# Expert outputs gate-scaled, split into a rounded head and a rounded rest, and summed into tokens by products with a 0/1 selection

## What is computed

```
logits = t @ w_router
top_val, top_idx = lax.top_k(logits, TOP_K)
gates = softmax(top_val)
combine = sum(one_hot(top_idx, N_EXPERTS) * gates[..., None], axis=1)
for e in range(N_EXPERTS):
    out = out + combine[:, e:e+1] * ((silu(t @ w_gate[e]) * (t @ w_up[e])) @ w_down[e])
x = x + out
```

## Time and profile before

| | us |
|---|---|
| three runs, median (lowest to highest) | 1259.38 (1258.75 to 1259.69) |
| the profiled execution, device time | 1258.63 |
| its span | 1256.9 |
| PE busy | 1230.5 (98%) |
| DVE busy | 574.3 (46%) |
| ACT busy | 435.2 (35%) |
| HBM rate over the span | 332 GB/s |

### The profile page before, as it was taken

One profiled execution on the slowest core, in us unless ns is written; L12 is line 12 of the kernel. 1 busy time (PEld: TensorE's weight loads), 2 busy tenths in 40 slices (PEclk: granted clock), 3 DMA queues, 4 the chain that ended last, 5 costly groups with the idle time before them and its releaser, 6 DMA issues.

```text
span 1256.9 us, 25739 instructions
## 1 busy us (share of the span) xinstructions
PE 1230.5 (98%) x11491; PEld 851.7 (68%) x11491; DVE 574.3 (46%) x898; ACT 435.2 (35%) x658; POOL 12.7 (1%) x38
## 2 busy tenths in 40 slices
PE   7999999999998999999999999999999999999997
PEld 6878888888877677777767877734366565544454
DVE  5786645556687556565765756502101011210103
ACT  6675534446564454354644544400000000000002
POOL 3000000000000000000000000000000000000000
PEclk9999999999998999999999999999999999999999
DMA  9646844165106999999999999999999999999992
GB/s 335 153 145 257 313 160 169 66 229 174 28 1 240 421 421 426 420 421 420 421 425 420 421 421 421 424 427 426 426 411 414 416 416 413 417 425 428 424 429 116
DMA packets 92773, 419.14 MB, mean 333 GB/s; under 512 B 4792, under 2 KB 8928, under 8 KB 84464
## 3 DMA queue, kind: packets, MB, share of 16 engines
q1 hardware_dynamic: 91456, 416.30, 82.1%
q0 software_dynamic: 640, 1.12, 0.4%
q10 hardware_dynamic: 560, 0.01, 0.0%
HBM read 416.37 MB, written 1.05 MB: 332 GB/s over the span
## 4 chain that ended last, share of the span: by engine, by line
PE 89%; DMA 7%; DVE 3%; ACT 1%; issue 0%; SPq 0%; DVEq 0%; ACTq 0%
PE bank L2387 26%; PE bank L2454 14%; PE bank L1983 14%; PE bank L1984 13%; PE bank L1985 13%; DMA ring<-in_moe_w_down 7%; PE bank L2321 2%; PE bank L2315 2%; DVE w_lo L1747 1%; PE bank L2049 1%; PE bank L2061 1%; PE bank L2073 1%; ACT w_hi L886 0%; DMA x<-in_x 0%; PE bank L2401 0%; PE bank L2254 0%
## 5 line engine op out<-in xcount | busy, mean ns | idle before, releaser
L1747 DVE TENSOR_TENSOR w_lo<-ring,w_hi 128x896 fp32r<-128x896 f32 (+2 forms) x192 | 201.8, 1089 | 75.2 <-ACT w_hi L886 69.7
L886 ACT ACTIVATE w_hi<-ring 128x896 fp32r<-128x896 f32 (+2 forms) x192 | 176.1, 948 | 121.8 <-PE bank L1985 95.0
L1163 ACT ACTIVATE silu_buf<-bank 128x448 f32<-128x448 f32 (+3 forms) x54 | 25.4, 485 | 407.0 <-PE bank L2387 407.0
L1983 PE MATMUL bank<-hi,act_hi 128*128 128x512 f32 (+1 forms) x400 | 154.4, 386 | 1.1 <-DVE lo L1293 1.1
L1984 PE MATMUL bank<-lo,act_hi 128*128 128x512 f32 (+1 forms) x400 | 152.5, 381 | 0.0
L1985 PE MATMUL bank<-hi,act_lo 128*128 128x512 f32 (+1 forms) x400 | 152.5, 381 | 0.0
L1770 DVE TENSOR_TENSOR silu_buf<-silu_buf,bank 128x448 f32<-128x448 f32 (+3 forms) x54 | 28.8, 550 | 233.3 <-PE bank L2387 212.1
L1293 DVE TENSOR_TENSOR lo<-raw_gu,hi 128x1024 fp32r<-128x1024 f32 x96 | 113.5, 1221 | 38.5 <-ACT hi L886 38.5
L2387 PE MATMUL bank<-ring,late_acts 128*32 128x448 f32 x1200 | 116.1, 539 | 0.0
L886 ACT ACTIVATE hi<-raw_gu 128x1024 fp32r<-128x1024 f32 x96 | 97.3, 1060 | 37.1 <-PE bank L1985 33.3
L2387 PE MATMUL bank<-ring,first_acts 128*32 128x224 f32 x2048 | 104.2, 354 | 0.6 <-ACT silu_buf L1163 0.6
(11 more groups left out here) (264 smaller groups left out, 1415.4 us busy)
## 6 DMA issues: line engine op xcount, KB each, us to landing
ring<-in_moe_w_down SPq DMA_DIRECT2D x58, 1792.0 KB, 19.6
ring<-in_moe_w_gate SPq DMA_DIRECT2D x57, 1792.0 KB, 18.0
ring<-in_moe_w_up SPq DMA_DIRECT2D x55, 1792.0 KB, 18.3
ring_after<-in_moe_w_up SPq DMA_DIRECT2D x9, 1792.0 KB, 14.4
raw_gu<-in_w_in SPq DMA_DIRECT2D x7, 2048.0 KB, 12.4
ring_after<-in_moe_w_down SPq DMA_DIRECT2D x6, 1792.0 KB, 12.2
ring_after<-in_moe_w_gate SPq DMA_DIRECT2D x6, 1792.0 KB, 13.0
raw_gu<-in_dense_w_gate SPq DMA_DIRECT2D x5, 2048.0 KB, 8.0
```

Of the source, the lines that this page charges most:

```text
L886: return nc.scalar.activation(out, in_, ACT.Copy, **kw)
L1163: nc.scalar.activation(out, gate, ACT.Silu).then_inc(e_silu_done, 1)
L1747: v.tensor_tensor(w_lo[:, n % WP, 0:b - a], flat(u)[:, a:b], w_hi[:, n % WP, 0:b - a], ALU.subtract).then_inc(w_lo_done, 1)
L1983: mm(out, ah, wh, start=start, stop=False, **kw)
```

## The change

Tile 0 of every pair, and tile 1 of pairs 0 and 1, are now *rounded* (`rounded_rows`); tile 1 of pairs 2 and 3 stays as it was. For rounded tiles:

- DVE's `gates` step compares instead of copying: `chosenT` is 1 where the transposed `gsel` is above 0, in the rounded type. The gate itself is had per slot: PE multiplies `gsel` with a column of ones (two float32 products with one column per tile), and DVE copies that column to `gate_slot`. In pair 0 this is done for both tiles at once.
- `rows_out` writes `yt_hi` = sum times gate, rounded (one tensor_scalar per old copy), waits for its own last write, and then writes `yt_lo` = sum times gate minus `yt_hi`, rounded (one scalar_tensor_tensor per old copy).
- `rows` makes two rounded products, `chosenT` by `yt_hi` and `chosenT` by `yt_lo`, instead of one float32 product.
- ACT no longer helps with the sums of the last pair's first member; DVE does all twelve pieces. ACT still helps with the second member.
- Some `extra` places of pairs 2 and 3 stand two places later. `at_buf` is smaller, and pair 2's first member keeps its activations in `late_acts` instead; no wait or instruction comes with that.

```diff
-        return ("rows", 0, n) if n < 4 else ("rows", 1, n - 6) if 6 <= n < 10 else ("gates", 0, 0) if n == 10 else None
+        return ("rows", 0, n) if n < 4 else ("rows", 1, n - 8) if 8 <= n < 12 else ("gates", 0, 0) if n == 12 else None
     if p == 3:
-        return ("rows", 0, n - 6) if 6 <= n < 10 else ("gates", n - 10, 0) if 10 <= n < 12 else None
+        return ("rows", 0, n - 8) if 8 <= n < 12 else ("gates", n - 12, 0) if 12 <= n < 14 else None
...
+def rounded_rows(p, tile):
+
+    return p < 2 or tile == 0
+
+
+def weighed_tiles(p, a):
+
+    return [t for t in ((0, 1) if p == 0 else (a,)) if rounded_rows(p, t)]
...
-                act.wait_ge(unit_used, last_unit("d", NS - 2) + 1)
-                for g in GROUPS[NP - 1, 0]:
-                    ins = last_rows_out(g)
-                ins.then_inc(y_last, 1)
...
-                        v.tensor_copy(gselT[0:m, a, :], bank[7][0:m, 0:SEQ]).then_inc(extra_out, 1)
+                        if rounded_rows(p, a):
+                            ins = v.tensor_scalar(chosenT[0:m, a, :], bank[7][0:m, 0:SEQ], 0.0, None, ALU.is_gt)
+                        else:
+                            ins = v.tensor_copy(gselT[0:m, a, :], bank[7][0:m, 0:SEQ])
+                        for tile in weighed_tiles(p, a):
+                            m, c = tile_rows(p, tile), SEQ + tile
+                            ins = v.tensor_copy(gate_slot[0:m, tile:tile + 1], bank[7][0:m, c:c + 1])
+                        ins.then_inc(extra_out, 1)
...
+                    for tile in sorted({part[1] for part in parts}):
+                        dve.wait_ge(extra_out, GATED[2 * p + tile])
+                    for rows, tile, cols, sums in parts:
+                        ins = v.tensor_scalar(yt_hi[rows, tile, cols], sums, gate_slot[rows, tile:tile + 1], None, ALU.mult)
+                    if len(parts) > 0:
+                        link(ins)
+                    for rows, tile, cols, sums in parts:
+                        ins = v.scalar_tensor_tensor(out=yt_lo[rows, tile, cols], in0=sums,
+                                                     scalar=gate_slot[rows, tile:tile + 1], in1=yt_hi[rows, tile, cols],
+                                                     op0=ALU.mult, op1=ALU.subtract)
...
-                    return mm(bank[b][:, :], gselT[0:m, tile, t * P:(t + 1) * P], yt[0:m, tile, c * 512:(c + 1) * 512],
+                    if rounded_rows(p, tile):
+                        mm(bank[b][:, :], chosenT[0:m, tile, tokens], yt_hi[0:m, tile, cols], start=start, stop=False)
+                        return mm(bank[b][:, :], chosenT[0:m, tile, tokens], yt_lo[0:m, tile, cols], start=False, stop=stop)
+                    return mm(bank[b][:, :], gselT[0:m, tile, tokens], yt[0:m, tile, cols],
...
+                        for tile in weighed_tiles(p, a):
+                            m, c = tile_rows(p, tile), SEQ + tile
+                            for t in range(NT):
+                                ins = mm(bank[7][0:m, c:c + 1], gsel[:, tile, t, 0:m], ones[:, 0:1], start=t == 0, stop=t == 1)
...
                 pe.wait_ge(y_out, 2 * NP - 1)
-                pe.wait_ge(y_last, 1)
-                pe.wait_ge(extra_out, EXTRA[NP - 1, 11])
+                pe.wait_ge(extra_out, EXTRA[NP - 1, 13])
                 for q, b in enumerate(LAST_BANKS):
                     rows(NP - 1, 0, q, b, True, False)
                 pe.wait_ge(y_out, 2 * NP)
-                pe.wait_ge(y_last, 2)
+                pe.wait_ge(y_last, 1)
```

More of the change, by code:

```diff
@@ L370 @@
             EXTRA[_p, _n] = len(EXTRA) + 1
+GATED = {extra_kind(*_k)[1] + 2 * _k[0]: _n for _k, _n in EXTRA.items() if extra_kind(*_k)[0] == "gates"}
+GATED[1] = GATED[0]
+def rounded_rows(p, tile):
+    return p < 2 or tile == 0
+def weighed_tiles(p, a):
+    return [t for t in ((0, 1) if p == 0 else (a,)) if rounded_rows(p, t)]
 GATHERED = {extra_kind(*_k)[2]: _n for _k, _n in EXTRA.items() if extra_kind(*_k)[0] == "gather"}
@@ L511, in build_trunk @@
         silu_buf = sb("silu_buf", [P, 3 * block_cols(NP - 1) // 4])
-        at_buf = sb("at_buf", [P, 3 * block_cols(NP - 1) // 4])
+        at_buf = sb("at_buf", [P, 3 * (BN // 4)])
         with ExitStack() as one:
@@ L516, in build_trunk @@
         at_late = sb("at_late", [P, 2048])
+        with ExitStack() as one:
+            yt_hi = sb_in(one, "yt_hi", [P, 2, D], F32R)
+            chosenT = sb_in(one, "chosenT", [P, 2, SEQ], F32R)
         yt = sb("yt", [P, 2, D])
@@ L521, in build_trunk @@
         nsink = sb("nsink", [P, 2, NH])
+        gate_slot = sb("gate_slot", [P, 2])
+        yt_lo = sb("yt_lo", [P, 2, D], F32R)
         last_acts = sb("last_acts", [P, KT * plain_slots(NP - 1)])
@@ L557, in e_at @@
                 return at_buf[:, n * w:n * w + n]
-            home = first_acts[0] if p == 1 else (at_late if w else at_buf)
+            home = first_acts[0] if p == 1 else (at_late if w else late_acts[1])
             return home[:, n * g.j:n * g.j + n]
@@ L1729, in rows_out @@
                 def rows_out(p, w, groups):
+                    parts = []
                     for g in groups:
                         if g.wide:
-                            ins = v.tensor_copy(yt[0:WIDE, 0, g.j * 512:(g.j + 1) * 512], bank[g.acc][:, :])
+                            rows, tile, cols = slice(0, WIDE), 0, slice(g.j * 512, (g.j + 1) * 512)
+                            parts.append((rows, tile, cols, bank[g.acc][:, :]))
                             continue
-                        if (p, w, g.j) == (NP - 1, 1, 1):
-                            dve.wait_ge(unit_used, N_UNITS)
-                        for c in range(2 if p == NP - 1 else 4):
-                            ins = v.tensor_copy(yt[g.row:g.row + 32, g.tile, c * 256:(c + 1) * 256],
-                                                bank[g.acc][32 * c:32 * c + 32, g.acc_col:g.acc_col + 256])
+                        for c in range(4):
+                            rows, tile, cols = slice(g.row, g.row + 32), g.tile, slice(c * 256, (c + 1) * 256)
+                            sums = bank[g.acc][32 * c:32 * c + 32, g.acc_col:g.acc_col + 256]
+                            if rounded_rows(p, tile):
+                                parts.append((rows, tile, cols, sums))
+                                continue
+                            if (p, w, g.j, c) == (NP - 1, 1, 1, 0):
+                                dve.wait_ge(unit_used, N_UNITS)
+                            if p < NP - 1 or c < 2:
+                                ins = v.tensor_copy(yt[rows, tile, cols], sums)
+                    for tile in sorted({part[1] for part in parts}):
[8 more added lines that the diff above has]
+                                                     op0=ALU.mult, op1=ALU.subtract)
                     ins.then_inc(y_out, 1)
@@ L2319, in rows @@
                 def rows(p, tile, q, b, start=True, stop=True):
-                    m, t, c = tile_rows(p, tile), q // 2, q % 2
-                    return mm(bank[b][:, :], gselT[0:m, tile, t * P:(t + 1) * P], yt[0:m, tile, c * 512:(c + 1) * 512],
+                    m, tokens, cols = tile_rows(p, tile), slice(q // 2 * P, q // 2 * P + P), slice(q % 2 * 512, q % 2 * 512 + 512)
+                    if rounded_rows(p, tile):
+                        mm(bank[b][:, :], chosenT[0:m, tile, tokens], yt_hi[0:m, tile, cols], start=start, stop=False)
+                        return mm(bank[b][:, :], chosenT[0:m, tile, tokens], yt_lo[0:m, tile, cols], start=False, stop=stop)
+                    return mm(bank[b][:, :], gselT[0:m, tile, tokens], yt[0:m, tile, cols],
                               start=start, stop=stop)
```

## The result

| | before | after |
|---|---|---|
| median of 20 runs each, us | 1259.68 (1258.75 to 1260.84) | 1262.18 (1259.71 to 1264.11) |
| ratio after / before | | 1.0018, 95% interval 1.0012 to 1.0024 |
| the profiled execution, its span, us | 1258.63, 1256.9 | 1260.37, 1258.7 |
| DVE busy, us | 574.3 | 604.1 |

The changed kernel is slower, by 0.18% in the ratio and by 2.5 us in the medians. The forecast was 1.5 us faster. Its 20 runs do not lie around one value: eight have a mean granted clock of 0.994 over the span and take 1260.46 us on average, nine have 0.992 and take 1263.28; the other three have 0.990, 0.991 and 0.993.

The account below looks back on a forecast made before the run. PE's row bounds the kernel behind 644 us, with the weight stream's end close behind. Handover +4.7, sums -6.4, gates +1.8 and end -1.6 make -1.5 us: 1257.9 us, range 1254.0 to 1261.3.

Parts of the forecast that it names:

- The two waits: Handover from pair 0 to pair 1: PE waits longer for DVE's `w_lo` and `at_wide_lo`, +2.3 and +3.8 us.
- The recovery in the down products: Down products behind the handover: with PE late, DVE no longer holds them up, 0.6 us back.
- the idle 0.78 us of before: PE's wait at 621.08 for ACT's SiLU, taken off the handover's first part, leaving +1.5 us.
- PE's rounded sums: Sums into tokens: two rounded products save 0.40 us each; 16 save 6.4 us in PE's row, the last 4 1.6.
- The slow rival: Rounded pairs: the second weight load isn't hidden, 20 pairs lose 3.8 us, giving 1261.7; 10%, with other such losses.
- The gates: Gates per slot on PE: 0.45 us per tile; four exposed tiles cost 1.8 us, pair 0's two are covered.
- The other handovers: Behind pairs 1 and 2: DVE's 3 and 8 us more are covered, costed at nothing.
- VectorE's operations: Sum times gate from PSUM, 256 columns: bounds 0.419 and 0.477 us, the upper taken; the rest's scalar_tensor_tensor 0.477.
- The end: Pair 3's first member: DVE takes 11.6 us, through at 1241.6, 0.3 us before PE wants it; PE saves 1.6.
- The rival that DVE is late there: Last pair's sums: DVE's 24 instructions average 0.55 us, the tail gains 0.3 instead of 1.6, giving 1259.2; 12%.
- The stream's end: Last load lands at 1234.4 us whatever PE does; gains ahead of the last down products are worth 3.8 us at most.
- The rival of a covered handover: Pair 0 to pair 1: PE really waits for the landing at 643.9, so the 4.7 us vanish, giving 1254.0; 13%.

Follow-up runs that it names:

- again: The changed kernel run once more with no edit; 1263.6 us, ratio 1.0031.
- fillers: The changed kernel with products of zeros into an unused bank in both PE waits of the pair 0 to pair 1 handover; 1259.05 us, ratio 0.9994.
- later: The changed kernel with DVE making the handover's second-part gated heads and rests behind both `at_wide_lo` pieces, not ahead; 1254.79 us, ratio 0.9962.
- both_later: `later` with the handover's first part also moved, behind all eight `w_lo` pieces of the gate weights instead of four; 1255.0 us, ratio 0.9959.

## Why the prediction was wrong

**The step that failed: that a wait costs its own length.** The two waits were forecast at +2.3 and +3.8 us and grew by 2.2 (2.39 for 0.16) and 3.7 (4.46 for 0.79). The place, the cause and the size were right. What was missing is that PE, having stood for them, can work at the 1.2 GHz level afterwards: the sum has no term for the clock. I had read the clock as 1.00 in all stretches of before, where the longer of these two waits was 0.79 us, and took it over unchanged for waits of 2.4 and 4.5. The trace of before had the sign, outside the stretches that I read. At 391.51 PE starts after 2.55 us of waiting (and little work in the 3 us ahead), and the clock is at its lower level; stretch of before, columns as in the earlier trace rows:

```profile
391.00:394.00 3.00, 2.49 (x8) 2.49 (x9) 2.31 (x14) 0.00 (x0) 0.00 (x0) 0.50 0.95 324
```

In the profile of after the low clock cost 0.3 us on the turn and 1.1 on the 192 narrow products; in that of `again` 0.3 and 2.5, and 1.5 behind the first wait. On the median it is the 3.1 us that `fillers` takes away. Forecast and result are 4.0 us apart on the two medians (-1.5 and +2.5); the clock is three quarters of it or a little more. `fillers` stands 0.85 us below the runs of before beside it, and its interval (-1.9 to +0.4 us) holds the forecast's -1.5.

The Trainium skill, "TensorE: Matmul & The Clock Gate", Part 1, The HAM clock gate, says that the clock gate's default is the throttled state and that activity releases it, and its Terms give the penalty as the throttled time times 1 - K/N, which is one half at that level. The traces agree with the first as far as they go: the level is low only where PE had stood still, but not behind every such wait. By the second the 0.66 over 4.7 us in after, 3.2 us at the low level, would be an estimated 1.6 us; the turn and the narrow products lost 0.28 + 1.10 = 1.4. The prediction used neither.

**The recovery in the down products: 0.4 us of the 0.6 came.** The lag is 7.45 us at the first wide down product (646.86) and 7.01 at the product at 653.13, behind the place where before waits 0.17 us for `w_lo`. Behind that, three sums of pair 0 save 1.2 and two tiles' gates cost 0.68, and yet the lag is 6.99 at 828.63: 0.4 us are lost on the way, between 694 and 820 us, in small steps spread over the wide down products. `later`, `both_later` and `fillers` lose the same 0.4 there. The prediction has no term for it, and its cause was not looked into. At the u weights the idle 0.78 us of before was taken off, rightly, for no bracket stands there in after.

**PE's rounded sums: right.** 0.39 us saved per pair in the row, forecast 0.40. The slow rival, that the second product's weights are not hidden, falls: the second record takes 0.23, and the next product follows at once. The Trainium skill, same page, Part 3, The mechanism, has it in its list of what overlaps that a weight load runs under products only where the row groups differ; for these loads, which the whole array takes, the trace's 0.23 does not agree.

**The gates: right, a little dear.** 0.34 us per tile where 0.45 was forecast; four tiles in the row cost 1.4 and not 1.8.

**Between 828 us and the end** PE gained 6.99 - 3.32 = 3.7 us. Twelve sums at 0.39 less two tiles at 0.34 are 4.0. The other handovers were costed at nothing, and that held to within the 0.3.

**VectorE's operations: right.** 0.48 us for 256 columns with the factor, as the bound that I took, and 0.48 for the rest.

**The end: right, with less room than I said.** The 24 instructions take 11.85 us. DVE is through at 1245.15 and PE starts the sums at 1245.26; the eight rounded ones take 1.96 us (forecast 1.83), and the lag falls from 3.32 to 1.8, thus by 1.5, forecast 1.6. The rival that DVE is late there did not come, but of the 0.3 us of room 0.1 was left.

**The stream's end: wrong as said, right in what followed.** I wrote that its 1234.4 us stays whatever PE does. It was 1238.7 in after: a PE that is 5 us late frees slots late, and the loads slip. It did not bind, since PE was late by more and used the last load some 3 us after landing. Where PE is early, in `later`, it stays at 1234.5, and PE uses the load 0.6 us after that. The floor that I had named was nearly reached there, and in no run met.

**The rival of a covered handover** was refuted as a description of this kernel, and was right about what lies behind it. In before, PE is within about a microsecond of being held by the landing at 643.9, and once the second wait is short or gone that landing sets its place (13.2 to 13.3 us behind it). In `later` the time is 1254.79, and that rival's price was 1254.0; that the two are so close is in part luck, since a first wait of 2.4 us still stands in `later` and the floor of 3.8 us was not what stopped it.

**Two slips in the working** change nothing in the forecast. With its own terms, 4.7 for the handover and 1.8 for the gates, 20 sums stop paying at a saving of 0.33 each and not 0.27. And 0.55 us off and 1.2 on make 1257.35 to 1259.1 and not 1256 to 1259.3.

What stays open: why the same waits bring one low stretch in some runs and more in others, why the first wait brings one in some profiles and none in others, and why the runs of `again` were all of the longer kind. What decides the level was not looked into.

## What to carry to other kernels

Price a new wait on TensorE as its length plus what may run behind it at the low clock, here 1.4 us in one profile and 4.3 in another behind waits of 2.4 and 4.5 us; a row in which the clock never fell says nothing of a kernel with longer waits, so look for the longest waits elsewhere in the same trace. When a change adds work to an engine that others keep pace with, look where in its order that work stands: here the same instructions brought no wait when they stood two places later, and the change turned from slower into 0.4% faster. And once the critical engine has gained a few microseconds, look for the next landing that it would meet before counting on more. Read places from that landing, since loads fall up to 1.7 us apart from profile to profile.

## What was unexpected in the hardware

- Products of zeros in a wait, useless in themselves, made the kernel 3.1 us faster by the granted clock alone.
- The same program with the same waits ran with a mean clock of 0.994 or of 0.992 from run to run, 2.8 us apart.
- A product with a per-partition factor, read from PSUM, costs as much as the operation with two operands and a factor: 0.480 us each for 256 columns, against 0.419 for the copy.
